# More of the early output projection in the level part of the last head, less in its recurrence

## The chip, the cores and the metric

The kernel runs on one core of a Trainium2 chip. The metric is device microseconds (us) of that core, start to end. TensorE (PE in the rows) does the matrix products, VectorE (DVE) and ScalarE (ACT) the elementwise work, GpSimd (POOL) a small part of it, and SyncE (SP) issues most transfers.

## The reference

One step of a two-layer decoder for 1024 prompt tokens and 8 sample tokens: a gated DeltaNet layer with 8 heads and then dilated-window attention, each followed by a squared-ReLU MLP. The change lies in the DeltaNet layer (`gdn_mixer`), at the end of its last head. Cut to what matters:

```python
T = triangular_solve(eye + lower, eye)           # per chunk: the "levels" of the kernel
...
def step(S, inp):                                # per chunk, in order: the "recurrence"
    v_new = u_c - w_c @ S
    o_c = qd_c @ S + a_c @ v_new
    S = S * dl_c + kd_c.T @ v_new
    return S, o_c
...
out = o.reshape(N, L, VAL_W_A) @ w_out           # the output projection, over all 8 heads
x = x + out
```

## The kernel before

Every matrix product of the projections and MLPs runs in float32 as three passes (high by high, low by high, high by low), so that one **k step** (128 of the contracted width, 128 output columns, one third of the 1032 tokens: 352, 352, 328) is three matmuls, L2266 to L2268 in the part of interest.

The eight heads run one after another. Each head has three parts. `front` builds scores and decays. `levels` inverts the chunk matrices in six levels, and each level has two halves: the first half (written 4.1 for level 4) begins with TensorE's small products of the level, which VectorE or ScalarE then copy out, and the second half (4.2) with the products that use them (L2358; in level 6 L2369 to L2371, "the corners", and L2376), which VectorE subtracts (L1583). `recurrence` goes through 8 chunks c; each has three **places** (24 in all, 0 to 23). In a chunk TensorE forms L2450 (state by k and by q), VectorE answers with L1660, TensorE forms L2458, VectorE answers with L1664, TensorE forms L2463 and L2466, VectorE answers with L1668 and L1674. Behind each of the three TensorE pieces comes a place, into which other work is put.

In heads 0 to 6 that other work is the input projection of the next head. The last head has no next head. There, the half levels from 2.1 on and the places carry the **early output projection**: the contribution of heads 0 to 3 to `out`, 18 products of 4 k steps each (72 steps, step m belongs to product m//4; after the recurrence steps 72 to 95 follow). Products alternate between two PSUM banks, 0 and 1. VectorE adds each finished product to x_half (L1436, function `early_product`), which frees its bank; product n+2 cannot start before product n was added. VectorE does this at a fixed place in its own order, one half level or place behind TensorE (`early_products`), and in a half level after the level's own VectorE work.

In the same stretch the last head also computes the recurrence of the 8 sample tokens. In levels 2 to 4 TensorE reads the old states (L2340), VectorE masks and reduces them (L1371, L1374), TensorE folds the result (L2347). The states and x_half are loaded on SP's queue after `front`. From level 6 on come 16 updates u, two for each of eight groups: GpSimd builds s_v_wide (L1062) and then scales the state (L1065); TensorE forms update 2g (L2246), VectorE adds it (L1421, which needs the scaled state), and only then may TensorE form update 2g+1, since both use bank 2. GpSimd starts the next group when update 2g+1 is formed. Updates 0 and 1 stand in 6.1 and 6.2, updates 2 to 15 at places 0 to 13, behind the k steps of the place. At chunk 1 VectorE also does `samples_out` (L1403 to L1408).

In level 5, between its subtraction and the added products, VectorE computes the norms of q: two reductions (L1594), L1597 and L1599. All engines run their own instructions strictly in the order written; nothing is reordered across these places. On TensorE a half level of the last head is:

```python
quads(3, 0, step, lambda rows, c, p: inv[rows, c, p]).then_inc(...)
...
if last and level > 1:
    early(early_done(2 * level - 5), early_done(2 * level - 4))
```

Of the kernel before, what the change touches and what calls it, by code (L numbers as in the profile page):

```python
# [68 lines left out]

def early_done(place):  # L70

    return max(2 * place + 2, 0) if place < 10 else min(20 + 52 * (place - 9) // 24, 72)


def dense_done(place):
# [96 lines left out]
def build(nc, t):  # L172
# [933 lines left out]
    def _(dve):  # L1106
# [316 lines left out]
        def early_products(place):  # L1423

            for n in range(early_done(place - 2) // UW, early_done(place - 1) // UW):
                early_product(n)
# [645 lines left out]
    def _(pe):  # L2072
# [307 lines left out]
        def levels(head):  # L2380
# [3 lines left out]
            for level in range(1, LEVELS + 1):  # L2384
# [15 lines left out]
                if last and level > 1:  # L2400
                    early(early_done(2 * level - 5), early_done(2 * level - 4))
# [22 lines left out]
                if last and level > 1:  # L2424
                    early(early_done(2 * level - 4), early_done(2 * level - 3))
# [446 lines left out]
```

## Time and profile before

| | |
|---|---|
| time, median of 3 runs | 2722.98 us (2721.94 to 2724.59) |
| the profiled execution's own time | 2721.97 us |
| its span | 2720.2 us |
| PE busy | 2638.9 us, 97% |
| DVE, ACT, POOL busy | 1553.1, 827.6, 66.6 us |
| levels and recurrence of the last head | about 628 to 737 us of the span |

The profile is one execution. The span runs from the first to the last instruction; the own time adds 1.8 us around it. The levels and recurrence of the last head are 4% of the span, and the only part in which the order of instructions differs.

### The profile page before, as it was taken

Reading aid. Unit: us, or ns where it says so; the run is one execution under the profiler, and the core shown is the slowest. Engines: PE = TensorE matmul, PEld = TensorE weight load, DVE = VectorE, ACT = ScalarE, POOL = GpSimd, SP = SyncE. Lnnn points to the kernel's source line nnn. Section 1 sums busy time; section 2 is a strip of 40 time slices with the busy share of each in tenths; the row PEclk is TensorE's granted clock in tenths of the full one; section 3 lists DMA queues with packets and bytes.
Section 4 is the critical chain, followed back from the end, with each engine's and each line's share of the span. In section 5 each row is a group of like instructions: output and inputs, shape, how many; then the busy total and the mean of one; then the engine's idle time right before and its main releaser. Section 6 shows DMA issues by size and latency. Waiting matters only on the chain.

```text
span 2720.2 us, 48302 instructions
## 1 busy us (share of the span) xinstructions
PE 2638.9 (97%) x20476; PEld 2508.2 (92%) x20476; DVE 1553.1 (57%) x2961; ACT 827.6 (30%) x1870; POOL 66.6 (2%) x92
## 2 busy tenths in 40 slices
PE   7999999997899999999999999988999999999998
PEld 6999999996699999999999998864899999999997
DVE  6777777777575444444444736567764444444445
ACT  5444544543141211121112314345531112111211
POOL 0000000000300000000000000002200000000000
PEclk9999999998999999999999999998999999999999
DMA  3111101134311111111111234334111111111111
GB/s 142 48 42 41 41 20 32 34 119 164 106 47 63 47 47 39 56 47 47 40 55 47 97 101 118 96 116 134 59 47 47 47 47 47 47 47 47 47 32 63
DMA packets 81989, 174.32 MB, mean 64 GB/s; under 512 B 21681, under 2 KB 46801, under 8 KB 81060
## 3 DMA queue, kind: packets, MB, share of 16 engines
q1 hardware_dynamic: 73860, 162.72, 18.5%
q10 hardware_dynamic: 7920, 8.56, 1.0%
q8 instruction: 162, 2.65, 0.4%
q14 instruction: 47, 0.39, 0.0%
HBM read 140.28 MB, written 36.21 MB: 65 GB/s over the span
## 4 chain that ended last, share of the span: by engine, by line
PE 89%; DVE 5%; DMA 2%; ACT 1%; issue 1%; POOL 1%; SPq 0%; DVEq 0%; ACTq 0%; POOLq 0%
PE psum L2085 19%; PE psum L2086 19%; PE psum L2087 19%; PE psum L2159 4%; PE psum L2160 4%; PE psum L2161 4%; PE psum L2111 2%; PE psum L2358 2%; PE psum L2609 2%; PE psum L2567 1%; PE psum L2632 1%; PE psum L2568 1%; PE psum L2569 1%; PE psum L2450 1%; DMA x_half<-in_x 1%
## 5 line engine op out<-in xcount | busy, mean ns | idle before, releaser
L2085 PE MATMUL psum<-x_hi,w_hi 128*128 128x352 f32 (+1 forms) x1040 | 334.8, 322 | 0.0
L2086 PE MATMUL psum<-x_lo,w_hi 128*128 128x352 f32 (+1 forms) x1040 | 332.4, 320 | 0.0
L2087 PE MATMUL psum<-x_hi,w_lo 128*128 128x352 f32 (+1 forms) x1040 | 330.9, 318 | 0.0
L1118 DVE SCALAR_TENSOR_TENSOR w_lo<-w_raw,gains,w_hi 128x512 fp32r<-128x512 f32 x380 | 262.1, 746 | 84.7 <-ACT w_hi L608 84.6
L608 ACT ACTIVATE w_hi<-w_raw,gains 128x512 fp32r<-128x512 f32 x380 | 246.9, 712 | 121.5 <-DMA w_raw<-in_w 121.2
L2159 PE MATMUL psum<-x_hi,w_hi 128*128 128x352 f32 (+1 forms) x768 | 273.2, 356 | 1.2 <-DVE pre L1200 1.2
L2085 PE MATMUL psum<-u_hi_b,w_hi 128*128 128x352 f32 (+1 forms) x768 | 247.1, 322 | 0.0
L2085 PE MATMUL psum<-u_hi,w_hi 128*128 128x352 f32 (+1 forms) x768 | 246.7, 321 | 0.0
L2085 PE MATMUL psum<-x_hi_b,w_hi 128*128 128x352 f32 (+1 forms) x768 | 246.6, 321 | 0.0
L2160 PE MATMUL psum<-x_lo,w_hi 128*128 128x352 f32 (+1 forms) x768 | 245.9, 320 | 0.0
L2086 PE MATMUL psum<-x_lo_b,w_hi 128*128 128x352 f32 (+1 forms) x768 | 245.5, 320 | 0.0
L2161 PE MATMUL psum<-x_hi,w_lo 128*128 128x352 f32 (+1 forms) x768 | 245.2, 319 | 0.0
L2087 PE MATMUL psum<-u_hi_b,w_lo 128*128 128x352 f32 (+1 forms) x768 | 245.2, 319 | 0.0
L2087 PE MATMUL psum<-u_hi,w_lo 128*128 128x352 f32 (+1 forms) x768 | 245.2, 319 | 0.0
L2086 PE MATMUL psum<-u_lo_b,w_hi 128*128 128x352 f32 (+1 forms) x768 | 245.0, 319 | 0.0
L2086 PE MATMUL psum<-u_lo,w_hi 128*128 128x352 f32 (+1 forms) x768 | 245.0, 319 | 0.0
L2087 PE MATMUL psum<-x_hi_b,w_lo 128*128 128x352 f32 (+1 forms) x768 | 244.3, 318 | 0.0
L1742 DVE SCALAR_TENSOR_TENSOR relu<-psum,rs 128x352 f32<-128x352 f32 (+1 forms) x192 | 99.1, 516 | 214.2 <-PE psum L2087 206.7
L908 ACT ACTIVATE u_hi_b<-relu 128x352 fp32r<-128x352 f32 (+1 forms) x96 | 47.2, 492 | 519.4 <-DVE relu L1745 519.4
L908 ACT ACTIVATE u_hi<-relu 128x352 fp32r<-128x352 f32 (+1 forms) x96 | 47.2, 492 | 516.8 <-DVE relu L1745 516.8
L2086 PEld LDWEIGHTS psum<-x_lo,w_hi 128*128 128x128 f32 x1040 | 195.5, 188 | 0.5
L2085 PEld LDWEIGHTS psum<-x_hi,w_hi 128*128 128x128 f32 x1040 | 195.4, 188 | 0.5
(373 smaller groups left out, 5542.4 us busy)
## 6 DMA issues: line engine op xcount, KB each, us to landing
w_raw<-in_w SPq DMA_DIRECT2D x190, 512.0 KB, 3.7
q_tile<-scratch_q SPq DMA_DIRECT2D x24, 256.0 KB, 3.0
scratch_att<-o_out ACTq DMA_DIRECT2D x32, 132.0 KB, 2.5
x<-in_x SPq DMA_DIRECT2D x8, 516.0 KB, 9.8
s_state<-in_s_rec_in SPq DMA_DIRECT2D x2, 2048.0 KB, 14.7
out_s_rec<-s_state SPq DMA_DIRECT2D x8, 512.0 KB, 2.6
merge<-scratch_att SPq DMA_DIRECT2D x8, 512.0 KB, 3.7
scratch_o_heads<-head_out ACTq DMA_DIRECT2D x7, 512.0 KB, 2.7
```

The lines of the kernel that those rows point to most:

```text
L608: done = act.activation(w_hi[:, slot, 2 * part + k], w_raw[:, part, k], ACT.Copy, scale=gains[:, unit * UW + 2 * part + k:unit * UW + 2 * ...
L908: act.activation(lay.u_hi[:, tile, THIRDS[third]], relu[:, 0:width(third)], ACT.Copy).then_inc(sem("u_hi_ready"), L.add("u_hi_ready"))
L1118: done = v.scalar_tensor_tensor(w_lo[:, slot, 2 * part + k], w_raw[:, part, k], gains[:, unit * UW + 2 * part + k:unit * UW + 2 * part + k ...
L1742: v.scalar_tensor_tensor(r, psum[:, TAKES[n % 6], 0:width(third)], 0.0, rs[:, cols], ALU.max, ALU.mult).then_inc(sem("product_free"), L.ad ...
L2085: mm(out, whi, xh[:, k, cols], start=k == 0, stop=False)
L2086: mm(out, whi, xl[:, k, cols], start=False, stop=False)
L2087: done = mm(out, wlo, xh[:, k, cols], start=False, stop=k == kts - 1)
L2111: done = nc.tensor.transpose(psum[0:cols, bank, at_col:at_col + rows], src, ident[0:rows, 0:rows])
L2159: mm(out, whi, x_hi[:, k, cols], start=k == 0, stop=False)
L2160: mm(out, whi, x_lo[:, k, cols], start=False, stop=False)
L2161: done = mm(out, wlo, x_hi[:, k, cols], start=False, stop=k == KT - 1)
L2358: done = mm(psum[out, bank + r, cols], lhs[rows, c, p], rhs(rows, c, p), start=True, stop=True, tile_position=(r * HD, c * HD))
```

## The change

`early_done(place)` says how many of the 72 steps are done when a half level or a place ends (half levels are numbers 0 to 9 and places 0 to 23 are numbers 10 to 33).

```diff
 def early_done(place):
 
-    return max(2 * place + 2, 0) if place < 10 else min(20 + 52 * (place - 9) // 24, 72)
+    return max(4 * place + 2, 0) if place < 10 else min(38 + 34 * (place - 9) // 24, 72)
```

Half level 2.1 keeps two steps; each of the nine from 2.2 to 6.2 takes four instead of two. So 38 steps stand in the levels instead of 20, and 34 in the 24 places (one or two each) instead of 52 (two or three each). In places 0 to 13 there are 19 instead of 30, in places 14 to 23 15 instead of 22. The number of instructions on every engine is the same. VectorE's additions move too, because they follow the same function.

TensorE at half level 5.2, before: the samples' last small products, the level's product L2358, then steps 14 and 15, then the corners of level 6.

```order
L2409 MATMUL psum<-ident,s_u 64x128
L2358 MATMUL psum<-dec,pair_79 64x64 [waits turned_ready,prod_ready]
L2358 MATMUL psum<-dec,pair_79 64x64 x15
L2266 MATMUL psum<-x_hi,w_hi 128x352
L2267 MATMUL psum<-x_lo,w_hi 128x352
L2268 MATMUL psum<-x_hi,w_lo 128x352
L2266 MATMUL psum<-x_hi,w_hi 128x352
L2267 MATMUL psum<-x_lo,w_hi 128x352
L2268 MATMUL psum<-x_hi,w_lo 128x352
L2369 MATMUL psum<-ident,pair_79 64x64 [waits steps_ready]
```

The same place after the change, from behind L2358 on: steps 26 to 29.

```order
L2266 MATMUL psum<-x_hi,w_hi 128x352
L2267 MATMUL psum<-x_lo,w_hi 128x352
L2268 MATMUL psum<-x_hi,w_lo 128x352
L2266 MATMUL psum<-x_hi,w_hi 128x352
L2267 MATMUL psum<-x_lo,w_hi 128x352
L2268 MATMUL psum<-x_hi,w_lo 128x352
L2266 MATMUL psum<-x_hi,w_hi 128x352 [waits product_free]
L2267 MATMUL psum<-x_lo,w_hi 128x352
L2268 MATMUL psum<-x_hi,w_lo 128x352
L2266 MATMUL psum<-x_hi,w_hi 128x352
L2267 MATMUL psum<-x_lo,w_hi 128x352
L2268 MATMUL psum<-x_hi,w_lo 128x352
```

Two steps were added ahead of the corners, and the first of them, step 28, opens product 7 and so waits for the bank of product 5.

VectorE in 5.2 and 6.1, before: the subtraction of the level, the norms of q, the copy of the corners, an added product, the addition of update 0, the last subtraction.

```order
L1583 TENSOR_TENSOR pair_79<-pair_79,psum 128x512 [waits steps_ready,step_full]
L1594 TENSOR_REDUCE col<-v_conv 128x4 [waits q_squares_ready]
L1594 TENSOR_REDUCE col<-v_conv 128x4
L1597 TENSOR_SCALAR col<-col 128x8 [waits dve_order]
L1599 RECIPROCAL col<-col 128x8 [waits dve_order]
L1564 COPY inv_t<-psum 64x8x64 [waits prod_full]
L1436 TENSOR_TENSOR x_half_116<-x_half_116,psum 128x352 [waits product_full,last_turned]
L1421 TENSOR_TENSOR s_state_113<-s_state_113,psum 128x512 [waits s_update0_full,s_scaled_ready]
L1586 TENSOR_SCALAR inv_t<-psum 64x8x64 [waits step_full]
```

The same after the change, from L1597 on.

```order
L1597 TENSOR_SCALAR col<-col 128x8 [waits dve_order]
L1599 RECIPROCAL col<-col 128x8 [waits dve_order]
L1436 TENSOR_TENSOR x_half_117<-x_half_117,psum 128x352 [waits product_full]
L1564 COPY inv_t<-psum 64x8x64 [waits prod_full]
L1436 TENSOR_TENSOR x_half_117<-x_half_117,psum 128x352 [waits product_full,last_turned]
L1421 TENSOR_TENSOR s_state_113<-s_state_113,psum 128x512 [waits s_update0_full,s_scaled_ready]
L1586 TENSOR_SCALAR inv_t<-psum 64x8x64 [waits step_full]
L1436 TENSOR_TENSOR x_half_117<-x_half_117,psum 128x352 [waits product_full]
```

The additions of products 5, 6 and 7 are the three L1436 rows; product 5 is added behind L1599. In the half levels there are now eight additions (products 0 to 7) instead of four.

## Rows read from the trace of the kernel before

**Rows 1.** The page, part 4: shares of the chain that ended last, by engine.

```profile
PE 89%; DVE 5%; DMA 2%; ACT 1%; issue 1%; POOL 1%; SPq 0%; DVEq 0%; ACTq 0%; POOLq 0%
```

**Rows 2.** Stretches of TensorE: us, busy us (instructions), granted clock, DMA share, GB/s.

```profile
656.61:659.38 2.77, 2.77 (x40) 0.50 0.00 0
744.60:748.20 3.60, 3.60 (x16) 0.55 0.00 0
642.90:649.30 6.40, 4.97 (x77) 0.50 0.99 421
679.32:722.36 43.04, 37.66 (x165) 1.00 0.33 122
722.36:734.82 12.46, 12.46 (x89) 1.00 0.17 56
```

**Rows 3.** Chain that ended last, in order of time: start us, us, what.

```profile
632.32 24.16 DMA x_half<-in_x
...
672.97 1.92 DVE col L1597
...
675.15 0.71 DVE inv_t L1564
...
716.78 1.89 POOL s_v_wide L1062
...
718.68 1.86 POOL s_state L1065
...
720.57 0.70 DVE s_state L1421
...
721.31 1.12 PE psum L2246 x2
```

**Rows 4.** Timeline, TensorE: start us, us, what [idle us before <- releaser].

```profile
656.61 1.93 PE L2340 MATMUL psum<-s_state,s_u 128*32 128x512 f32 x8 [2.11 <-DMA x_half<-in_x]
...
669.35 0.43 PE L2407 MATMUL psum<-s_u,ones 128*128 128x64 f32 x2 [0.65 <-DVE s_u L1397]
...
670.30 0.69 PE L2358 MATMUL psum<-dec,pair 64*64 64x64 f32 x32
...
675.99 1.11 PE L2376 MATMUL psum<-inv_t,dec 64*64 64x64 f32 x16 [0.53 <-DVE inv_t L1564]
...
678.20 1.12 PE L2246 MATMUL psum<-s_v_wide,s_rows 64*128 64x512 f32 x2
...
695.46 0.32 PE L2266 MATMUL psum<-x_hi,w_hi 128*128 128x352 f32 x1
...
695.94 0.32 PE L2266 MATMUL psum<-x_hi,w_hi 128*128 128x352 f32 x1
...
725.28 0.38 PE L2458 MATMUL psum<-vz,inv_t 128*128 128x128 f32 x2
```

**Rows 5.** Timeline, VectorE.

```profile
671.06 0.69 DVE L1583 TENSOR_TENSOR pair<-pair,psum 128x512 f32<-128x512 f32 x1 [1.76 <-PE psum L2358]
...
675.88 0.52 DVE L1436 TENSOR_TENSOR x_half<-x_half,psum 128x352 f32<-128x352 f32 x1
...
725.70 0.35 DVE L1664 TENSOR_SCALAR vz<-psum,col 128x128 f32<-128x128 f32 x1 [0.63 <-PE psum L2458]
...
731.64 1.41 DVE L1118 SCALAR_TENSOR_TENSOR w_lo<-w_raw,gains,w_hi 128x512 fp32r<-128x512 f32 x2
...
735.50 0.49 DVE L1436 TENSOR_TENSOR x_half<-x_half,psum 128x328 f32<-128x328 f32 x1
```

**Rows 6.** Timeline, GpSimd.

```profile
672.96 1.89 POOL L1065 TENSOR_TENSOR s_state<-s_state,s_gate 128x1024 f32<-128x1024 f32 x1
...
697.72 1.89 POOL L1062 TENSOR_TENSOR s_v_wide<-ident,s_rows 64x1024 f32<-64x1024 f32 x1 [2.54 <-PE psum L2246]
...
704.69 1.89 POOL L1062 TENSOR_TENSOR s_v_wide<-ident,s_rows 64x1024 f32<-64x1024 f32 x1 [3.19 <-PE psum L2246]
```

**Rows 7.** Line L1597, all eight heads: ns minimum/median/maximum, first and last start.

```profile
L1597 DVE TENSOR_SCALAR col<-col x8: 170/172/1906, 109.9 to 673.0; 128x8 f32<-128x8 f32 x8
```

## The prediction

> **What bounds the kernel now.** I read the shares of the chain first: TensorE holds 89% of it [rows 1]. So a change that only moves TensorE's work can gain only where TensorE waits, and its k steps cost their full length wherever it doesn't. Then I read the stretch of the change in the table of stretches, and there the answer differs from part to part.
>
> - Levels 2 and 3 end at a transfer. The chain holds 24.16 us of the load of x_half, issued at 632.32 [rows 3], and TensorE's read of the second half of the states waits 2.11 us for it at 656.61 [rows 4].
> - Levels 4 to 6 are a hand-to-hand of TensorE and VectorE with small gaps: 0.65 us before L2407, 0.53 us before L2376 [rows 4].
> - Places 0 to 13 go at GpSimd's pace. The stretch 679.32 to 722.36 has 37.66 us of TensorE work in 43.04 [rows 2], and the chain runs through GpSimd and VectorE [rows 3]: L1062 at 716.78, L1065 at 718.68, L1421 at 720.57, update at 721.31.
> - Places 14 to 23: TensorE is busy all of 12.46 us [rows 2].
>
> **The price of a step.** Two first matmuls of neighbouring steps start at 695.46 and 695.94 [rows 4]: 0.48 us a step. 18 steps move, so 8.6 us of TensorE work. If both sides were bound by TensorE the sum would be 0.
>
> **Levels 2 and 3: six added steps, 0.** Two each in 2.2, 3.1 and 3.2. The two of 2.2 lie ahead of an earlier wait for a transfer; the four of level 3 are 1.92 us and fit in the 2.11 us wait [rows 4]. VectorE's additions of products 0 and 1 need only the first states, long landed. Cover gone, these steps would cost up to 2.9 us; the transfer is issued before anything that changes, so I keep 0.
>
> **The clock after that wait: -0.9 us.** The granted clock is 0.50 from 656.61 to 659.38 [rows 2], that is 1.2 instead of 2.4 GHz, after the idle 2.11 us. Filled with steps, TensorE should not fall. The read L2340 takes 1.93 us there [rows 4], and at the full clock half, about 1.0. What is behind it (VectorE's masking, then the fold) follows. Bounds: 0 to -1.4 (half of 2.77).
>
> **4.1 and 4.2: +0.96 each.** The samples' read in 4.1 and the fifth level behind 4.2 stand behind the steps, with no wait to hide in. **5.1: +0.3**, which is 0.96 less the 0.65 us that L2407 waits now [rows 4]. With the clock's -0.9 the start of 5.2 comes 1.3 us later.
>
> **5.2: a new wait, the main term.** Step 28 needs product 5 added, and that addition stands behind the norms of q in VectorE's order. Now L1583 starts at 671.06 [rows 5], L1597 at 672.97 and takes 1.92 us, and L1564 can only start at 675.15 [rows 3], 4.1 us after L1583. In seven heads L1597 takes 0.17 us and in this one 1.906 [rows 7]; it starts as GpSimd's L1065 starts (672.96) and ends as that ends at 674.85 [rows 6]. GpSimd's start follows L2409 in 5.1, which moves with the same 1.2 us or so, so L1597 should meet L1065 again. TensorE has two steps (1.0 us) to do behind L2358 (670.30 [rows 4], end 0.6 us later), then stands about 3.3 us.
>
> This is why it isn't hidden. Before, TensorE did the corners, two steps and update 0 while VectorE was at the norms, and still waited 0.53 us at L2376: L2376 started 0.84 us after L1564 (675.15 to 675.99). After, all this comes behind the norms. From the end of L1599 to L2376: addition of product 5, 0.55 (0.52 a piece [rows 5]); steps 28 and 29, 0.96; corners, 1.1; the copy L1564, 0.7; addition of product 6, for which step 32 waits, 0.5; steps 32 and 33, 1.05; update 0, 1.1 (1.12 [rows 4]). That is 6.0 instead of 0.84, **+5.1 us**, on top of the +1.2 with which L1599 ends.
>
> The Trainium skill (SBUF — State Buffer, SBUF: two separate sides) calls the port pair that VectorE and GpSimd share an exclusive lock, held for a whole instruction, the loser blocked. Rows 6 and 7 agree: L1597 ends with L1065. By that rule the hold-up stays as long as L1065 begins first; were the two to miss each other, the stall would be 1.7 us shorter.
>
> **The clock after the stall: +1.3 us.** After the long wait that ends at 744.60 the clock is 0.55 for 3.60 us [rows 2], a loss of 1.6 to 1.8 us. The stall in 5.2 is about as long as that one. Part of the loss falls on VectorE's time, so I take 1.3; bounds 0 and 3.2 (6.40 us at 0.50 from 642.90 to 649.30 [rows 2], where TensorE also had gaps between its work).
>
> The Trainium skill (TensorE: Matmul & The Clock Gate, HAM oscillation — how this bites in real kernels) says that a wait inside a loop sends the array back to half rate and the work behind it runs cold. By it the stall costs more than its own length, as above; without it the sum is 1.3 lower.
>
> **6.2: +1.1.** Two steps, and 0.15 of waiting for product 7 (L1586 and the addition, 1.2 us, against two steps of 1.0). Update 1 (678.20 to 679.32 [rows 4]) then ends 1.2 + 5.1 + 1.3 + 1.1 = **8.7 us later**.
>
> **Places 0 to 13: eleven steps fewer, -1.9 only.** A group of updates cannot be faster than L1062 1.89, L1065 1.86, L1421 0.70 and the update 1.12 with handoffs: 716.78 to 722.43 is 5.65 [rows 3], 5.7 to the next start. Seven groups are now 43.04 [rows 2]. One of them, 697.72 to 704.69 [rows 6], takes 6.97, since `samples_out` fills VectorE, and its place 7 keeps two steps. So 6 x 5.7 + 6.97 = 41.2, a gain of 1.9. The other 3.4 us of the removed steps become waits for GpSimd. Bounds: 0 and -5.3.
>
> **Places 14 to 23: -2.3.** Six of the seven steps lie before the last L2463, 2.9 us. A handoff costs 0.42 (L2458 at 725.28 to L1664 at 725.70 [rows 4, 5]), 0.35 and 0.05, so 0.8; with one step a gap it shows once, 0.2. In chunk 6 VectorE has the weight split L1118 of 1.41 [rows 5] in the chain, which costs 0.35 once TensorE is faster. Left: 2.3. **The end: -0.4**, because no product is added in place 23 (the 0.49 us row at 735.50 [rows 5]), where VectorE's chain leads to the next stage.
>
> **Sum**: 8.7 - 1.9 - 2.3 - 0.4 = +4.1 us. Against the profiled execution's 2721.97 that is 2726.1; its own time is 1.0 below the median 2722.98, so 2727.0.
>
> **The rivals.** About 0.2% (5.4 us) is what a measurement of this kernel can tell from no change.
>
> - *Forecast*: the stall in 5.2 and one clock fall. 2725.8 to 2728.3. Chance 0.48.
> - *A shorter stall*: the clock holds (-1.3), or L1597 escapes L1065 (-1.7). For it: the clock stays at 1.00 through many gaps of 1 us. Against: 3.3 us is as long as gaps that brought it down. 2725.3 to 2725.7, both 2724. Chance 0.17.
> - *Slower, by a half clock that stays through level 6*: after the stall TensorE's work is cut by waits for products 6 and 7 and for L1564, as from 642.90 to 649.30. Place: from step 28 to update 1. Price: 3.2 instead of 1.3, so +6.0, 2728.9. It decides if the clock is still at half when update 0 starts. The same comes of no gain at 656.61 together with any stretch over 2 us at half. Chance 0.20.
> - *No stall*: product 5's addition is in time. Then 5.2 and 6.1 cost 0.96 each less the 0.53 wait, update 1 ends 3.7 late, and the sum is -1.0: 2722.0. Against: the order of VectorE. Chance 0.07.
> - *Faster*: no stall, and all 18 steps come back in the places at 0.48 (-8.6), GpSimd's pace not binding: 3.7 - 8.6 - 0.4 = -5.3, 2717.7. Against: the chain through L1062 and L1065. It decides if TensorE is still the last at the even updates. Chance 0.05.
> - The rest, 0.03, is something unseen.
>
> **How the numbers follow.** Time 2727.0, the likeliest case. The first three cases and "no stall" span 2722.0 to 2729; with the bounds of the clock terms 2722.0 to 2730.0 should hold the time 8 times in 10. The likeliest case's own range is 2725.8 to 2728.3. Slower by over 0.2% is the third case and the upper edge of the first: 0.23. Faster: 0.06. The same: 0.71.
>
> **What would show it.** Right: in 5.2 a wait of about 3 us before an L2266, released by VectorE's L1436 behind L1599; a granted clock near 0.5 behind it; no clock fall at 656; waits for POOL L1062 and for L1421 in all groups, with the groups 5.7 us apart; update 1 about 8 to 9 us later; levels 2 and 3 unchanged in time. Wrong: a wait at step 28 under 1 us, a read of the second states later than 657, or groups still 6.2 us apart. What would make the prediction wrong most easily is the clock, in either place.

## The result, and the profile after

The changed kernel takes 2734.3 us (median of 8 runs, 2729.37 to 2741.57), beside 2722.85 us (8 runs, 2720.56 to 2727.36) for the kernel before on the same chip: ratio 1.0041, 95% interval 1.0032 to 1.0050. It is slower by about 11 us. The prediction was 2727.0 with a range of 2722.0 to 2730.0.

The profiled execution took 2738.49 us, 4.2 over the median, with a span of 2736.7, so it is 16.5 us of span longer than that of before. Page, part 1, of the changed kernel (busy us, share of the span, instructions):

```profile
PE 2653.5 (97%) x20476; PEld 2517.6 (92%) x20476; DVE 1554.2 (57%) x2961; ACT 828.3 (30%) x1870; POOL 66.6 (2%) x92
```

TensorE has the same 20476 instructions as before, and is busy 14.6 us longer. So most of the loss isn't waiting: the same matmuls took longer. Where, the stretches of TensorE in the changed kernel show (us, busy us, instructions, granted clock, DMA share, GB/s):

```profile
656.00:658.60 2.60, 2.13 (x72) 1.00 0.03 6
675.96:679.60 3.64, 3.64 (x54) 0.54 0.00 0
687.96:738.38 50.42, 43.91 (x133) 0.75 0.28 104
709.60:720.10 10.50, 10.50 (x28) 0.52 0.13 51
720.10:723.50 3.40, 2.47 (x10) 0.97 0.08 31
723.50:740.50 17.00, 16.80 (x38) 0.51 0.17 69
738.38:749.61 11.23, 11.05 (x71) 0.89 0.18 54
```

The first line answers to the 0.50 at 656.61 [rows 2]: the clock no longer falls there. The second is the fall that was expected behind the stall in 5.2. The third is places 0 to 13 (end of update 1 to end of update 15), 50.42 us where before had 43.04 [rows 2]. It holds 32 instructions of TensorE less (eleven steps are 33, and a record may be missing). The clock is the reason that it is longer: 10.5 us at 0.52 and then 17 us at 0.51, both almost wholly at the 1.2 GHz level. In the last of these TensorE is busy 16.80 of 17.00 us.

TensorE's own timeline shows how each fall begins (start, length, line, and in brackets the wait before it and who ended it):

```profile
655.97 1.06 PE L2340 MATMUL psum<-s_state,s_u 128*32 128x512 f32 x8 [0.89 <-DMA x_half<-in_x]
...
675.96 0.66 PE L2266 MATMUL psum<-x_hi,w_hi 128*128 128x352 f32 x1 [3.36 <-DVE x_half L1436]
...
707.17 1.12 PE L2246 MATMUL psum<-s_v_wide,s_rows 64*128 64x512 f32 x2 [0.91 <-POOL s_v_wide L1062]
...
709.60 0.49 PE L2458 MATMUL psum<-vz,inv_t 128*128 128x128 f32 x2 [1.31 <-DVE vz L1660]
...
720.55 1.12 PE L2246 MATMUL psum<-s_v_wide,s_rows 64*128 64x512 f32 x2
...
723.70 2.07 PE L2246 MATMUL psum<-s_v_wide,s_rows 64*128 64x512 f32 x2 [1.13 <-POOL s_v_wide L1062]
...
728.61 2.07 PE L2246 MATMUL psum<-s_v_wide,s_rows 64*128 64x512 f32 x2
```

The first line is the cover in level 3: the wait for x_half's load is 0.89 us where it was 2.11, and the read takes 1.06 instead of 1.93 us. Step 28 waits 3.36 us at 675.96. The two falls in the places begin at waits of 1.31 us (ends at 709.60) and 1.13 us (ends at 723.70), and an update takes 2.07 us in them instead of 1.12. The wait of 1.31 us behind L1660 is where `samples_out` holds VectorE. The kernel before has the very same wait, and its clock stays at 1.00:

```profile
702.10 0.49 PE L2458 MATMUL psum<-vz,inv_t 128*128 128x128 f32 x2 [1.31 <-DVE vz L1660]
```

VectorE in 5.2 and 6.1 of the changed kernel, which answers to [rows 5]:

```profile
671.50 0.69 DVE L1583 TENSOR_TENSOR pair<-pair,psum 128x512 f32<-128x512 f32 x1 [1.80 <-PE psum L2358]
...
673.41 1.87 DVE L1597 TENSOR_SCALAR col<-col 128x8 f32<-128x8 f32 x1
...
675.43 0.47 DVE L1436 TENSOR_TENSOR x_half<-x_half,psum 128x352 f32<-128x352 f32 x1
679.81 0.69 DVE L1564 COPY inv_t<-psum 64x512 f32<-64x512 f32 x1 [3.91 <-PE psum L2371]
```

The addition for which step 28 waits stands behind L1597, which is held for 1.87 us, and then VectorE itself stands 3.91 us for the corners. GpSimd of the changed kernel, which answers to [rows 6]:

```profile
673.36 1.89 POOL L1065 TENSOR_TENSOR s_state<-s_state,s_gate 128x1024 f32<-128x1024 f32 x1
688.04 1.89 POOL L1062 TENSOR_TENSOR s_v_wide<-ident,s_rows 64x1024 f32<-64x1024 f32 x1 [12.79 <-PE psum L2246]
...
693.77 1.89 POOL L1062 TENSOR_TENSOR s_v_wide<-ident,s_rows 64x1024 f32<-64x1024 f32 x1 [1.98 <-PE psum L2246]
...
713.86 1.89 POOL L1062 TENSOR_TENSOR s_v_wide<-ident,s_rows 64x1024 f32<-64x1024 f32 x1 [4.86 <-PE psum L2246]
...
721.75 1.89 POOL L1062 TENSOR_TENSOR s_v_wide<-ident,s_rows 64x1024 f32<-64x1024 f32 x1 [4.14 <-PE psum L2246]
...
730.76 1.89 POOL L1062 TENSOR_TENSOR s_v_wide<-ident,s_rows 64x1024 f32<-64x1024 f32 x1 [5.26 <-PE psum L2246]
```

The first groups start 5.73 us apart, as forecast for GpSimd's pace. From 705.22 on they are 8.64, 7.89 and 9.01 us apart, and the wait is for TensorE's update.

The 16.5 us of span, by the same instructions in both profiles: start to the second read of the states -0.6; from there to the end of update 1 +9.3 (655.97:687.96 against 656.61:679.32); places 0 to 13 +7.4; places 14 on to the last L2463 -1.2 (11.23 us); to L2111 at 759.10 -0.3; after it +2.0 (each rounded by itself). L2111 is the first product of the stage behind the recurrence. What follows it is the same code in all kernels here; it takes 1973.7 to 1977.9 us over their profiles, and 1975.9 in a second profile of the changed kernel (1975.6 before), so it isn't the change's. The second read of the states, too, starts anywhere from 655.6 to 659.6 us over the profiles, with the steps ahead of it or without. So profiles are best compared over what lies between, from this read to L2111: 87.99 us before (656.61 to 744.60), 103.13 in this profile of the changed kernel and 100.31 in its second.

### The profile page after: what moved, and what is told of

Read it like the earlier page. It is cut to its first block, busy times and chain, and to the rows that moved or that the text cites. A ratio compares the mean times of both kernels' runs of the same rounds, so it can differ in the third digit from the quotient of the medians.

```text
span 2736.7 us, 48301 instructions
## 1 busy us (share of the span) xinstructions
PE 2653.5 (97%) x20476; PEld 2517.6 (92%) x20476; DVE 1554.2 (57%) x2961; ACT 828.3 (30%) x1870; POOL 66.6 (2%) x92
## 4 chain that ended last, share of the span: by engine, by line
PE 88%; DVE 5%; DMA 2%; ACT 1%; issue 1%; POOL 1%; SPq 0%; DVEq 0%; ACTq 0%; POOLq 0%
PE psum L2085 19%; PE psum L2086 19%; PE psum L2087 19%; PE psum L2159 4%; PE psum L2160 4%; PE psum L2161 4%; PE psum L2358 2%; PE psum L2111 2%; PE psum L2609 2%; PE psum L2567 1%; PE psum L2568 1%; PE psum L2569 1%; PE psum L2632 1%; PE psum L2450 1%; DMA q_tile<-scratch_q 1%
```

## The experiments

Two theories. **A**: the places with 19 steps instead of 30 bring the clock down. **B**: the stall in 5.2 does, and the lean places alone don't. The kernel before, timed beside each group on its chip: 2724.06, 2723.1, 2723.29 and 2722.78 us (23 to 30 runs each). The stretch of places 0 to 13 is given for each profile, from the end of update 1 to the end of update 15, us and granted clock, and in the last column the stretch from the second read of the states to L2111 (87.99 us before). Time and ratio are of many executions, the last two columns of one.

| kernel | stall | steps in 0-13 | time, us (range, runs) | ratio to before (95%) | 0-13, clock | read to L2111 |
|---|---|---|---|---|---|---|
| add5_first | no | 19 | 2726.21 (2721.32-2737.63, 11) | 1.0011 (0.9998-1.0024) | 43.04, .96 | 90.36 |
| places_full | yes | 30 | 2728.76 (2726.18-2730.78, 11) | 1.0016 (1.0007-1.0025) | 42.40, 1.00 | 93.93 |
| lean_places | no | 19 | 2725.63 (2722.27-2730.39, 11) | 1.0007 (0.9998-1.0016) | 44.09, .94 | 91.28 |
| steps_doubled | yes | 19 + 9 rep. | 2735.79 (2733.96-2737.19, 5) | 1.0039 (1.0026-1.0053) | 47.73, .86 | 99.19 |
| add5_and_full | no | 30 | 2723.47 (2721.47-2728.51, 11) | 1.0001 (0.9992-1.0010) | 42.37, 1.00 | 88.93 |
| doubled_to_30 | yes | 19 + 11 rep. | 2732.26 (2729.95-2735.54, 8) | 1.0030 (1.0020-1.0041) | 43.10, 1.00 | 94.56 |
| places_28 | yes | 28 | 2729.18 (2727.52-2733.40, 11) | 1.0023 (1.0014-1.0032) | 44.80, .92 | 95.26 |
| hidden_only | no | 30 | 2720.78 (2716.33-2724.26, 11) | 0.9990 (0.9981-0.9999) | 45.10, .92 | 86.40 |
| changed_again | yes | 19 | 2737.41 (2735.67-2739.27, 5) | 1.0050 (1.0037-1.0063) | 47.94, .82 | 100.31 |
| add5_doubled | no | 19 + 11 rep. | 2728.62 (2724.12-2733.61, 11) | 1.0020 (1.0011-1.0029) | 45.70, .93 | 93.00 |
| leaner_places | no | 15 | 2731.02 (2729.19-2734.93, 6) | 1.0030 (1.0018-1.0042) | 47.59, .82 | 93.49 |
| hidden_again | no | 30 | 2721.97 (2718.76-2723.65, 11) | 0.9990 (0.9982-0.9999) | 45.09, .92 | 86.34 |
| out_late | yes | 19 | 2727.51 (2725.08-2735.41, 11) | 1.0015 (1.0006-1.0024) | 45.24, .84 | 98.83 |
| hidden_out_late | no | 30 | 2718.47 (2715.72-2720.39, 11) | 0.9983 (0.9974-0.9992) | 41.26, 1.00 | 83.02 |
| all_doubled | yes | 19, each twice | 2731.55 (2728.32-2733.52, 7) | 1.0026 (1.0015-1.0037) | 47.27, .96 | 98.59 |
| before_out_late | no | 30 | 2720.86 (2719.48-2724.48, 11) | 0.9993 (0.9984-1.0002) | 41.85, 1.00 | 86.84 |

**The first two: the stall gone, and the places full.** Product 5's addition goes ahead of the norms of q; and, apart from it, the changed levels with the old density in the places.

```diff
 # add5_first
+                if last and level == 5:
+                    early_products(7)
...
-                if last and level > 1:
+                if last and level > 1 and level != 5:
# places_full
-    ... else min(38 + 34 * (place - 9) // 24, 72)
+    ... else 38 + 30 * (place - 9) // 14 if place < 24 else min(68 + 4 * (place - 23) // 10, 72)
```

> The changed kernel, with one edit: VectorE adds product 5 ahead of the norms of q in half level 5.2 instead of behind them. Both theories expect the 3.36 us wait before step 28 to vanish and update 1 to end 4 to 6 us earlier than in the changed kernel (about 682 to 684 instead of 687.9). Theory A (the rest of the loss is TensorE's clock, which falls in places 0 to 13 because too few steps are left there, whatever happened before): the clock still falls to half in places 0 to 13, and the time is 2726 to 2731, slower than the kernel before. Theory B (the stall in 5.2 is what brings the clock down, and the falls in the recurrence are its echo): with the stall gone the clock holds, and the time is 2721 to 2723.

> The changed kernel's levels (38 steps, the stall in 5.2 included), but places 0 to 13 keep the 30 steps that they had before, and places 14 to 23 have the last 4. Theory A: the clock stays at 1.00 from update 1 on through place 13, that stretch takes about the 43.0 us of before instead of 50.5, and the time is 2724 to 2729, several us under the changed kernel's 2734. Theory B (the stall's echo): the clock falls in places 0 to 13 as in the changed kernel, about 2733. Not clear in either: places 14 to 23 have almost no steps, so the clock could fall there.

Stretches of add5_first, places 0 to 13 and the fall in them:

```profile
683.74:726.78 43.04, 34.16 (x133) 0.96 0.33 122
716.70:720.10 3.40, 3.40 (x12) 0.54 0.00 0
```

Stretches of places_full, places 0 to 13 and from there to the last L2463:

```profile
689.30:731.70 42.40, 37.46 (x166) 1.00 0.34 125
731.70:741.06 9.36, 6.80 (x40) 1.00 0.21 64
```

Each has one half of the trouble. add5_first has no stall and update 1 ends at 683.74; yet its places take the same 43.04 us as before although 11 steps are gone, and two of its 11 runs took 2735.84 and 2737.63. places_full has the whole stall (3.36 us) and the slow clock behind it, and still no fall at all in the profile of its places: B alone can't be the whole.

**Lean places in the kernel before, and repeats in the changed one.** In lean_places 11 of the 30 steps are skipped. In steps_doubled nine steps of places 0 to 13 are run twice into the same bank (start and stop off), so that TensorE has the work of 28 steps.

```diff
 # lean_places, on the kernel before
+                if m in (21, 22, 26, 29, 30, 33, 37, 41, 45, 46, 49):
+                    continue
# steps_doubled, on the changed kernel
+                if m in (38, 39, 42, 45, 46, 49, 52, 55, 56):
+                    mm(out, whi, x_hi[:, k, cols], start=False, stop=False)
+                    mm(out, whi, x_lo[:, k, cols], start=False, stop=False)
+                    mm(out, wlo, x_hi[:, k, cols], start=False, stop=False)
```

> The kernel before, levels untouched, but 11 of the 30 k steps of places 0 to 13 are left out altogether (steps 21, 22, 26, 29, 30, 33, 37, 41, 45, 46 and 49; the output lacks their share), so that each place has about as many steps as in the changed kernel. 5.3 us of TensorE work less. Theory A: slower than the kernel before in spite of less work, by 4 to 10 us (2727 to 2733), with the granted clock at 0.5 in parts of places 0 to 13 and a wide spread between executions. Theory B and my prediction's step (places 0 to 13 go at GpSimd's pace at full clock): 1.9 us faster, 2721.

> The changed kernel, but in each of the nine places of 0 to 13 that have one k step its three matmuls are issued twice (steps 38, 39, 42, 45, 46, 49, 52, 55, 56; the output counts their share twice). 4.3 us of useless TensorE work more, nothing else changed. Theory A: the clock holds in places 0 to 13, and the time falls from 2734 to 2725 to 2729. Theory B, or if the places were just short of time: no faster than the changed kernel, 2734 to 2738.

Stretches of lean_places (places 0 to 13, and two falls in and behind them):

```profile
679.56:723.65 44.09, 35.06 (x133) 0.94 0.32 119
694.60:698.00 3.40, 3.40 (x11) 0.54 0.00 0
721.80:728.60 6.80, 6.80 (x22) 0.51 0.19 77
```

With no stall and nothing moved, 5.3 us less work, the kernel is not faster but 1.6 us over before (interval up to +4.4): A's mechanism is there without a stall, but smaller than A's 2727 to 2733; the time lies between the two forecasts. steps_doubled missed: with 28 steps' worth it fell all the same, 0.55 over 711.60:726.90, and was about as slow as the changed kernel.

**Both repairs; more repeats; real steps to 28; only the hidden steps.** add5_and_full joins the first two. doubled_to_30 is steps_doubled with 11 repeats. places_28 puts two real steps in each of places 0 to 13 and 6 in the rest. hidden_only takes four steps in 2.2, 3.1 and 3.2 alone, where the wait for x_half covers them:

```diff
 # places_28
+    ... else 38 + 2 * (place - 9) if place < 24 else min(66 + 6 * (place - 23) // 10, 72)
# hidden_only
+    half = (2, 6, 10, 14, 16, 18, 20, 22, 24, 26)
+    if place < 10:
+        return half[place] if place >= 0 else 0
+    return 26 + 30 * (place - 9) // 14 if place < 24 else min(56 + 16 * (place - 23) // 10, 72)
```

> Both edits together: product 5 is added ahead of the norms in 5.2, and places 0 to 13 keep 30 steps. If the loss of the changed kernel is the stall (with its clock fall) plus the clock in lean places, and the two add up, this takes about 4.5 to 5 us off the 2728.8 of the version with full places: 2724, within 0.1% of the kernel before, and with the narrow spread of that version. If the stall and the lean places matter only together, it is the same as either alone, 2726 to 2729.

> The changed kernel with eleven repeats of the three matmuls of a step in places 0 to 13 (steps 38, 39, 42, 45 twice, 46, 49, 52, 53, 55, 56), so that every place has as many matmuls as before: 30 steps' worth against 28 in the run with nine repeats, which didn't help. The output counts their share again. If two steps' worth more or less decides whether the clock holds, 2727 to 2730. If repeats don't do what real steps do, or the place in time of the stall decides, about 2735 as with nine.

> As the version with full places (stall in 5.2 included), but exactly two real steps in each of places 0 to 13, 28 instead of 30, and six in places 14 to 23. If two steps decide, the clock falls as with nine repeats: 2733 to 2736. If real steps do what repeats do not, 2728 to 2729 as with 30.

> The kernel before, but four steps only in half levels 2.2, 3.1 and 3.2, ahead of the two waits for transfers (six more steps there), the other half levels two as before, places 0 to 13 their 30, and the six taken from places 14 to 23 (16 instead of 22). By the account of the waits: six steps hidden, 2.0 to 2.9 us back in places 14 to 23, and up to 1 us from the clock that no longer falls at 656, so 2719.5 to 2721.5 against 2723 to 2724 before. If instead every cut of steps in the recurrence brings the clock down, 2723 or slower.

add5_and_full is at the time of before (ratio 1.0001), and no fall is in its places. VectorE there:

```profile
672.74 0.69 DVE L1583 TENSOR_TENSOR pair<-pair,psum 128x512 f32<-128x512 f32 x1 [1.81 <-PE psum L2360]
673.35 0.52 DVE L1436 TENSOR_TENSOR x_half<-x_half,psum 128x352 f32<-128x352 f32 x1
...
675.08 1.44 DVE L1599 TENSOR_SCALAR col<-col 128x8 f32<-128x8 f32 x1
```

The addition starts 0.61 us behind L1583, where it was 3.93 us. Between places_full, 2728.76, and add5_and_full, 2723.47, lies the stall alone: 5.3 us, or 4.3 if each is taken against the kernel before of its own group (4.7 less 0.4). Their profiles, from the read to L2111, differ by 5.0. doubled_to_30 (2732.26) met neither of its forecasts. It shows no fall in its places, yet its median is 3.1 us over that of places_28, which does show one. Its repeats were taken from nowhere, so that places 14 to the last L2463 take 10.11 us against 9.36 in places_full; that is 0.8 of the 3.5 us between it and places_full. The profile doesn't show the rest as a cost of the repeats: from the read to L2111 it takes 94.56 us, 0.6 more than places_full and 0.7 less than places_28. This execution was slow (2733.06) in code that the edit doesn't touch: the read comes at 658.83 instead of 656.62 in places_full, and what follows L2111 takes 1977.9 instead of 1975.2. One profile can't say what the others of its executions did, and the intervals of doubled_to_30 and places_28 overlap. hidden_only is 2.3 us faster than before, and even it, with all 30 steps, has a fall in its places (703.10:709.90 at 0.50, busy 6.80 of 6.80).

**Two kernels timed again, and the dose.** changed_again is the changed kernel once more; add5_doubled is add5_first with 11 repeats; leaner_places leaves 15 of the 30 steps of the kernel before out; hidden_again is hidden_only once more.

```diff
 # leaner_places, on the kernel before
+                if 20 <= m < 50 and k in (1, 2):
+                    continue
```

> The changed kernel once more, unedited, for a second profile and its spread beside the runs of this group. If the clock falls in places 0 to 13 are what makes it slow, its slow stretches lie elsewhere or last otherwise than in the first profile, while the waits of levels 2 to 6 come out the same within 0.3 us; median 2732 to 2736, with a spread of about 10 us again.

> The changed kernel with product 5 added ahead of the norms (no stall) and with the eleven repeats in places 0 to 13 (30 steps' worth; the output counts their share again). If lean places bring the clock down with no stall before them, and the amount of dense work decides, the repeats take away the executions of 2735 to 2738 that the version without repeats had, and the median is 2723.5 to 2725.5 against 2726.2, with 5.3 us of useless work more. If the amount of work doesn't matter, the spread stays and the median is 2726 or more.

> The kernel before, levels untouched, with all second and third steps of each product left out in places 0 to 13: 15 of 30 remain, 7.2 us of TensorE work less (the output lacks their share). If less dense work makes the clock fall more, this is slower than the version with 11 steps left out (2725.6): 2727 to 2735. If falls are a matter of chance with one step a place or of the stall, 2723 to 2726. By GpSimd's pace at full clock 2721.

> The version with four steps only in 2.2, 3.1 and 3.2 once more, to see whether its gain of 0.1% holds: 2720 to 2722 against 2723 to 2724 of the kernel before. If the first result was chance, 2723 or more.

Stretches of changed_again, the slow clock behind the stall, places 0 to 13 and the main fall in them:

```profile
679.51:685.79 6.28, 6.28 (x62) 0.50 0.00 0
692.31:740.25 47.94, 39.96 (x133) 0.82 0.30 110
713.30:726.90 13.60, 12.94 (x31) 0.51 0.10 39
```

Stretches of leaner_places, the same:

```profile
683.29:730.88 47.59, 37.53 (x121) 0.82 0.30 111
703.10:716.70 13.60, 11.80 (x29) 0.50 0.12 48
```

In changed_again the slow clock behind the stall lasts over 6 us, where the first profile had 3.64, and places 0 to 13 take 2.5 us less; its time is above the forecast of 2732 to 2736, and its five runs spread over 3.6 us and not over 10.

leaner_places is the clearest run of the study. It is the kernel before with 7.2 us of TensorE work (15 steps at 0.48) taken out and nothing put anywhere, and it is 7.7 us slower (by the interval of its ratio, 4.9 to 11.4). In its profile 5.5 us of that lie between the read and L2111, 4.5 of them in places 0 to 13; the rest isn't the edit's. The medians go 2724.1 and 2723.3 (all 30 steps, both groups), 2725.6 (19), 2731.0 (15). TensorE has less to do and gets less clock to do it at. add5_doubled isn't better than add5_first (2728.62 and 2726.21): without the stall repeats bring nothing. hidden_again repeats hidden_only's gain, and TensorE's timeline shows where its fall begins (701.40:709.90 at 0.60):

```profile
702.07 0.49 PE L2461 MATMUL psum<-vz,inv_t 128*128 128x128 f32 x2 [1.31 <-DVE vz L1663]
```

**The trigger.** That 1.31 us wait for `samples_out` is where the falls begin, within it or up to about 1 us behind it, in both profiles of the changed kernel, in steps_doubled, places_28, hidden_only, hidden_again and add5_doubled. In add5_first, lean_places and leaner_places the first fall begins instead behind a wait for GpSimd's L1062, of 1.13, 1.13 and 1.38 us, during the update that waited or at its end. What was open was whether it is needed for them. In three of the next kernels `samples_out` and the store behind it stand three chunks later; all_doubled runs each of the 19 steps of places 0 to 13 twice.

```diff
 # out_late, hidden_out_late, before_out_late
-                    if place == 3 and c == 1:
+                    if place == 3 and c == 4:
...
-                    if place == 3 and c == 2:
+                    if place == 3 and c == 5:
# all_doubled
+                if 38 <= m < 57:
+                    mm(out, whi, x_hi[:, k, cols], start=False, stop=False)
...
```

> The changed kernel (stall included) with VectorE's samples_out moved from chunk 1 to chunk 4 and output_samples from 2 to 5, behind all updates. In two profiles of the changed kernel the clock falls right at the wait of 1.31 us that samples_out causes before L2458 of chunk 2. If that wait is what tips the clock in lean places, the fall is gone or shorter and the median drops from 2734 to 2737 down to 2727 to 2731, of which only 1.2 us are the wait itself. If the leanness alone does it, 2732 to 2736.

> The version with four steps only in 2.2, 3.1 and 3.2, with samples_out and output_samples moved as in the run beside it. Its two profiles had a clock fall of 7 to 8 us beginning at the same wait. Expected 2718 to 2720 against 2721 to 2722 without the move: 1.2 us for the wait and 1 to 2 us for the clock, less what samples_out costs in chunk 4. If the wait doesn't matter for the clock, 2720.5 to 2721.5.

> The changed kernel with all 19 steps of places 0 to 13 issued twice (the output counts them twice): 38 steps' worth, more than the 30 of before, 9.1 us of useless work more than the changed kernel. If dense work holds the clock, whoever it is for, places 0 to 13 take 43 to 44 us at full clock in every execution and the median is 2729 to 2732. If repeats do not hold it, 2736 or slower.

> The kernel before with samples_out and output_samples moved alone. By the waits: one group of updates takes 5.8 instead of 6.97 us, and samples_out in chunk 4 costs TensorE up to 1 us, so 0 to -1.2 us; by the clock, if some executions of the kernel before also fall there, a narrower spread and 1 us more. 2721 to 2723.

Stretches of out_late, in its slowest execution (2735.41 us; the median is 2727.51):

```profile
690.08:720.10 30.02, 24.58 (x102) 1.00 0.39 140
720.10:738.80 18.70, 17.99 (x46) 0.54 0.21 85
```

The row of TensorE's timeline in that execution at which the clock falls:

```profile
720.81 1.90 PE L2246 MATMUL psum<-s_v_wide,s_rows 64*128 64x512 f32 x2 [1.13 <-POOL s_v_wide L1062]
```

Stretches of hidden_out_late, places 0 to 13 and from there to the last L2463:

```profile
676.44:717.70 41.26, 37.62 (x166) 1.00 0.34 128
717.70:729.26 11.56, 11.17 (x74) 1.00 0.19 57
```

Moving `samples_out` takes 7 to 10 us off the changed kernel (2734.3 and 2737.4 to 2727.5), 2.9 off hidden_only (mean of 2720.8 and 2722.0; 1.9 if each is taken against the kernel before of its own group) and 1.9 off the kernel before, whose interval reaches 1.0002. The group of updates in which it stood took 6.97 us [rows 6], and the other six of the kernel before 6.0 on the average; with it moved, places 0 to 13 of the kernel before are 1.2 us shorter (41.85 us) at the same clock of 1.00. So about 1.2 us is the wait. That the rest is the clock is shown for hidden_only, whose places go from 45.10 us at 0.92 to 41.26 at 1.00. For the changed kernel it is argued, since the only profile of out_late is of its slowest execution. The wait isn't the only trigger: in that profile the clock stays at 1.00 over the old place and falls at about 721.0, behind a wait of 1.13 us for GpSimd that ends at 720.81. all_doubled has 9.1 us more TensorE work (19 steps at 0.48) than the changed kernel and is 3 to 6 us faster; its places still have a short fall (0.96 over all), so the 43 to 44 us expected became 47.27. With the stall, 0, 9, 11 and 19 repeats give ratios of 1.0041 and 1.0050, 1.0039, 1.0030 and 1.0026. The medians fall as the work in the places grows, though neighbours overlap in their intervals, and even the first and the last touch. hidden_out_late, 0.9983 (0.9974 to 0.9992), has the lowest median of all.

## Why the prediction was wrong

What held, by its own steps:
- **Levels 2 and 3, 0, and the clock after that wait, -0.9.** The wait went from 2.11 to 0.89 us and the clock stayed at 1.00. hidden_only and hidden_again, which of the changed levels have this part alone (and six steps fewer in places 14 to 23), are 2.3 and 1.3 us faster than before.
- **5.2, the new wait.** 3.3 forecast, 3.36 measured, by the instruction named; L1597 1.87 us beside L1065. The stall with its clock fall (0.54 over 3.64 us) was priced at +5.1 and +1.3; with and without it the forecasts lay 5.0 apart (2727.0 and 2722.0), and the runs (places_full and add5_and_full) 4.3 to 5.3.
- **Update 1 8.7 us later.** It is 8.6 later on the clock of the profile, and 9.3 counted from the second read of the states. The fall is there at 0.54 and gone by 679.60, before update 0 starts at 682.28, so the rival of a half clock through level 6 didn't happen. The one clock fall of 3.6 us was partly luck: in the profiles of changed_again, places_full and out_late it lasts over 6 us, and from the read to the end of update 1 they take 0.7 to 0.8 us more than the first profile. It ends before update 0 there too.
- **Places 14 to 23, -2.3**, came to -1.2, at clock 0.89 since the fall reaches to 740.50; in changed_again, where it doesn't, to -2.2. **The end, -0.4**, came to -0.3.
- **The sums.** Three are 0.1 off, and nothing hangs on it: 2721.97, 1.0 and 4.1 make 2727.1, the case of no stall sums to -0.9, and the start of 5.2 is put 1.3 us later but goes into the sum as 1.2. It measured 1.1, counted from the second read.

The step that failed is **"Places 0 to 13: eleven steps fewer, -1.9 only"**, with bounds of 0 and -5.3. It measured +7.4 us in the first profile and +4.9 in changed_again. Its pace was right as long as the clock held: 5.73 us a group where 5.7 was forecast. The fault is that the 3.4 us of removed steps were let "become waits for GpSimd" at no price, with TensorE taken at full clock. The prediction priced the clock in two other places, at the wait in level 3 and behind the stall, and named it as what could fail "in either place", but not in this one, where TensorE lost the most work. Gaps of this length come up only in the rival of a shorter stall: "the clock stays at 1.00 through many gaps of 1 us". That was true of places with 30 steps [rows 2], and nothing in the prediction asked whether it holds with 19.

What stands in its place: two causes that meet. The lean places cost by themselves. leaner_places shows it, with an interval wholly above 1 (1.0018 to 1.0042) and a clock of 0.82 in its places. lean_places and add5_first point the same way and prove it less: the one has 1 in its interval, the other is 2.7 us over add5_and_full with intervals that overlap. By the forecast's terms add5_first should have been 1.1 us under it (-1.9 and -2.3, against the -3.1 that places_full measured behind its places). With the stall ahead of them the same leanness costs 5.5 us (2734.3 less places_full's 2728.76) and 8.7 by changed_again, so the two together cost 3 to 6 us more than the sum of each alone; with intervals of 2 to 4 us to either side that excess is likely and not shown beyond doubt. And where the clock falls is mostly the `samples_out` wait: without it the changed kernel takes 2727.5 us. That this is 0.5 from the forecast is in part luck, as the forecast still held the 1.2 us of that wait. The forecast lacked the price of the clock in the places; its account of the order and of the waits held.

The Trainium skill (TensorE: Matmul & The Clock Gate, HAM oscillation — how this bites in real kernels) lays the falls in its example to waits for transfers, each longer than any wait in these places. By that section alone the clock wouldn't fall in the places. The runs say otherwise: it fell at waits of 1.13 to 1.38 us.

What stays open. Whether repeats of a step help less than real steps: the median of doubled_to_30 says so, its profile doesn't, and add5_doubled is no better than add5_first. Whether it is the stall that makes the fall longer that begins some 30 us behind it, and how: leaner_places has one of 13.6 us without a stall. And what sets it for a single execution: the changed kernel's runs spread over 12 us, add5_first's over 16.

## What to carry to other kernels

Ask of every stretch that gets less work, not only of the one that gets more, what else that work did: here it kept TensorE's clock up while another engine set the pace, and taking 7.2 us of it out made the kernel 7.7 us slower (leaner_places). Move work to where a transfer is waited for, but leave a stretch that goes at another engine's pace as full as its pace allows. When a product has to wait for a bank, look at what the engine that frees it does first: one addition put ahead of the norms took the whole stall away.

## What the hardware showed that wasn't expected

TensorE can stay at 1.2 GHz while hardly idle: 16.80 of 17.00 us busy at 0.51 (723.50:740.50), 10.50 of 10.50 at 0.52, and 6.80 of 6.80 at 0.50 in hidden_only, in stretches made of the sample updates L2246 and of small matmuls with one to three k steps between. The same mix at 1.00 is busy 24.58 of 30.02 us (out_late). So once the clock is down, the slower work fills the waits, and a busy TensorE doesn't show that it is fast; only the granted clock does. And the same wait of 1.31 us brought the clock down in one kernel and left it up in another, both with 19 steps around it (changed, add5_first) and with 30 (hidden_only, before).
